# Routing slots by one-hot products, the first token gathers in the routing stage, and three embedding tiles and a prepared weight for the last stage of a hybrid transformer block

## The chip, the cores and the metric

One Trainium2 chip; the program runs on one of its cores. The metric is the device time of one execution in microseconds (us). The kernel before took 3019.23 us, the median of three executions (3015.76 to 3023.67). Each execution computes the whole block once, in float32 data, for 2048 tokens of width 1024.

## The reference

One layer of a decoder block: three token mixers side by side (a gated linear attention, a sparse attention that picks 256 keys, a sliding window), an output product, then a hierarchical mixture of experts, then a per-token embedding that is gated by the hidden state, and a last norm. The change touches only what follows the output product:

```python
h = h + hier_moe(rms_norm(h, g_ffn), ...)         # 4 groups of 8 experts, the best 2 in one group
e = rms_norm(p @ w_ple, g_ple)                    # p: 2048 x 256, w_ple: 256 x 1024
h = h + e * sigmoid(h @ w_ple_gate)               # w_ple_gate: 1024 x 1024
out = rms_norm(h, g_final)
```

Inside `hier_moe` each token's two expert choices are sorted by expert and every expert's tokens are padded to whole blocks of 128. `row` is the place of a (token, choice) pair in that padded list, and each block of 128 rows goes through `silu(xb @ w_gate[e]) * (xb @ w_up[e])` and then `@ w_down[e]`. The kernel so needs both directions of the map: from a token to its two rows (to fetch its results), and from a row to its token (to fetch its input, called its slot).

## The kernel before, in words

The program is a row of stages. Each is a block in which the five engines run their own instruction streams, tied by semaphores, and the stages are parted by a barrier of all engines. The last four are `mix` (output product, h and the normed f to memory, router logits), `route`, `experts` and `finish`. A tile is 128 tokens, so there are 16.

**route** (L1859 to L2118). VectorE (DVE) turns the logits into gates, into `rows` (L2089, a tile that holds each token's two rows) and then into `blocks`, the table of experts and counts that the later stages read into registers. TensorE (PE) ranks the tokens by two products with a triangle and with ones (L2019, L2020), between the products for tile 2 and tile 3 (`RANKED_AT`). Beside this, PE and ScalarE (ACT) compute the embedding `p @ w_ple` for all 16 tiles: PE turns a tile of p (L1996) and multiplies it (L2007), ACT squares the result for the norm (L1967), copies it (L1970) and stores it to `e_dram` (L1972). GpSimd (POOL) writes the slots by 32 indirect transfers (L1949) that scatter token numbers into `slots_dram`, one for each tile and choice, and it waits for all of them. SyncE (SP) loads p and the first experts' weights (`prefetch`, L2144 and L2149): gate and up for two experts and two down matrices, the second of which waits for the first to land.

**experts** (L2152 to L2431). For each block of 128 rows: POOL loads its slots from `slots_dram` (L2239), gathers 128 rows of f (L2247), PE turns them (L2311), ACT copies them to a rounded half, POOL makes the remainder (L2255), and PE does gate and up as three rounded products each (L2323 to L2325: high by high, low by high, high by low), then turns the hidden rows (L2332) and does down in full float32 (L2341). DVE splits each expert's gate and up into a rounded half `high` (L2232) and the remainder, in place, in `low` (L2234). The two buffers of `low` alternate by expert. The loop over blocks is a hardware loop whose count comes from `blocks`; `low` and `wd` are addressed there by a register. SP loads the next weights as buffers come free and at last `w_ple_gate` into `wg` (`load_next`, L2443).

**finish** (L2446 to L2661). It begins with ACT rounding `wg` to `wg_high` (L2592) and DVE making `wg_low` (L2647). For each tile: SP loads h and e, POOL gathers its two rows of results y (L2518), DVE adds them with their gates (L2611), PE turns the sum (L2546), ACT and DVE split it (L2576, L2620), PE does 48 products of 512 columns (L2558 to L2560), ACT takes the sigmoid (L2583), DVE multiplies and adds (L2633, L2635), ACT squares (L2588), POOL takes the inverse root, DVE scales (L2641) and SP stores. The order on PE is turn(0), turn(1), product(0), turn(2), product(1) and so on. Tile 0's products wait for all of tile 0's split, and each k of them for its slice of `wg_low`.

## Time and profile before

| | us |
|---|---|
| median of three executions | 3019.23 |
| the profiled execution | 3013.49 |
| its span, first to last instruction | 3011.8 |
| `mix` ends, `route` begins | 1705.0 |
| `route` ends, `experts` begins | 1791.4 |
| `experts` ends, `finish` begins | 2785.0 |
| PE busy in the span | 2668.7 (89%) |
| DVE, ACT, POOL busy | 1799.7, 1287.6, 985.0 |
| memory read and written | 331.69 MB, 107.53 MB |

The stage borders are read from the start of the first instructions of each stage in the trace. A span's engine share says little here, since each stage has its own limit: read the time at which a stage's last wait ends, what ended it, and what PE does in the first microseconds of the next stage.

### The profile page before, as it was taken

How to read it: one execution, taken by the hardware profiler on the slowest of the kernel's cores; microseconds unless marked ns; L12 is line 12 of the kernel's file. 1: busy time of each engine (PE TensorE's matmuls, PEld its weight loads, DVE VectorE, ACT ScalarE, POOL GpSimd, SP SyncE). 2: the span in 40 equal slices, each digit the busy share in tenths (PEclk: the TensorE clock that was granted, in tenths of full speed). 3: DMA queues.
4: the chain of work that ended last, by engine and by line, in shares of the span. 5: the costliest groups of instructions: out<-in, count | busy, mean ns of one | idle time of the engine just before them, and what ended most of it. 6: DMA issues, size and time to landing. Idle time of an engine off the chain costs nothing. (4 is left out here: it accounts for less than half of the span.)

```text
span 3011.8 us, 34857 instructions
## 1 busy us (share of the span) xinstructions
PE 2668.7 (89%) x11056; PEld 1674.1 (56%) x11057; DVE 1799.7 (60%) x2255; ACT 1287.6 (43%) x2377; POOL 985.0 (33%) x973
## 2 busy tenths in 40 slices
PE   6989789999947878888799869999999999998698
PEld 3634333444833434444588626666666666665587
DVE  2188999688876666766322346764564445740676
ACT  2377868839815556665222242222222222222222
POOL 1477887200011111121000054534544445441221
PEclk9999999999978989999799889999999999999799
DMA  5102211111141123212444486996596665971564
GB/s 154 50 29 52 33 34 39 56 56 54 39 129 57 43 65 104 67 50 91 179 146 148 179 206 242 325 361 211 204 346 219 216 218 205 347 282 42 206 227 140
DMA packets 224946, 440.79 MB, mean 146 GB/s; under 512 B 25704, under 2 KB 93864, under 8 KB 224696
## 3 DMA queue, kind: packets, MB, share of 16 engines
q1 hardware_dynamic: 199528, 357.78, 34.8%
q0 software_dynamic: 16080, 47.93, 5.1%
q10 hardware_dynamic: 9216, 33.56, 3.2%
q8 instruction: 63, 1.03, 0.1%
q14 instruction: 59, 0.48, 0.1%
HBM read 331.69 MB, written 107.53 MB: 146 GB/s over the span
## 5 line engine op out<-in xcount | busy, mean ns | idle before, releaser
L2232 DVE CAST p_high<-p_low 128x2048 fp32r<-128x2048 f32 x128 | 200.9, 1569 | 441.0 <-PE p_psG L2325 300.1
L625 PE MATMUL p_psP<-home,p_ring 128*128 128x512 f32 (+1 forms) x960 | 421.0, 597 | 0.0
L2341 PE MATMUL p_psY<-p_wd,p_hT 128*128 x768 | 337.9, 593 | 2.1 <-ACT p_hT L2401 1.9
L2234 DVE TENSOR_TENSOR p_low<-p_low,p_high 128x2048 fp32r<-128x2048 f32 x128 | 319.8, 2499 | 4.4
L625 PEld LDWEIGHTS p_psP<-home,p_ring 128*128 128x128 f32 (+1 forms) x960 | 175.4, 185 | 241.0 <-issue 240.8
L2261 POOL TENSOR_TENSOR p_hid<-p_act_g,p_act_u 128x512 f32<-128x512 f32 x48 | 62.0, 1292 | 528.3 <-ACT p_act_u L2396 276.2
L2341 PEld LDWEIGHTS p_psY<-p_wd,p_hT 128*128 128x128 f32 x768 | 142.2, 190 | 163.7 <-issue 163.5
L654 PE MATMUL p_psI<-p_kI,p_qI 64*128 64x512 f32 (+3 forms) x608 | 147.8, 594 | 54.2 <-ACT p_relu L550 54.1
L2255 POOL TENSOR_TENSOR p_xT_low<-p_xT,p_xT_high 128x512 fp32r<-128x512 f32 x96 | 191.1, 2008 | 1.5 <-ACT p_xT L2386 1.5
L2323 PE MATMUL p_psG<-p_high,p_xT_high 128*128 128x512 f32 x384 | 170.7, 445 | 15.6 <-DVE p_low L2234 9.3
L698 DVE TENSOR_SCALAR_CACHE_REDUCE p_equal<-p_S_low,p_flip 128x512 uint8<-128x512 f32 (+4 forms) x139 | 168.6, 1213 | 0.0
L2323 PE MATMUL p_psU<-p_high,p_xT_high 128*128 128x512 f32 x384 | 157.4, 410 | 5.2 <-DVE p_low L2234 5.2
L564 ACT ACTIVATE p_relu<-p_relu,p_small 128x512 f32<-128x512 f32 (+3 forms) x266 | 161.4, 661 | 0.0
L550 ACT ACTIVATE p_relu<-p_psI 128x1024 f32<-128x1024 f32 (+3 forms) x152 | 136.7, 914 | 40.5 <-POOL p_S_high L481 14.6
L2407 ACT ACTIVATE p_y<-p_psY 128x512 f32<-128x512 f32 x96 | 57.4, 598 | 224.7 <-PE p_psY L2341 224.7
L2325 PE MATMUL p_psG<-p_high,p_xT_low 128*128 128x512 f32 x384 | 153.2, 399 | 0.0
L2324 PE MATMUL p_psG<-p_low,p_xT_high 128*128 x384 | 153.2, 399 | 0.0
L698 DVE TENSOR_SCALAR_CACHE_REDUCE p_above<-p_S_low,p_flip 128x384 uint8<-128x384 f32 (+4 forms) x139 | 150.5, 1083 | 3.3
L2324 PE MATMUL p_psU<-p_low,p_xT_high 128*128 x384 | 151.9, 396 | 0.0
L2325 PE MATMUL p_psU<-p_high,p_xT_low 128*128 128x512 f32 x384 | 151.8, 395 | 0.0
L1330 PE MATMUL p_psL<-p_kA,home 64*128 64x512 f32 (+3 forms) x320 | 85.1, 607 | 69.0 <-ACT home L1216 32.4
L1473 DVE SCALAR_TENSOR_TENSOR p_logits<-p_mask,p_psL 128x1024 f32<-128x1024 uint8 (+3 forms) x80 | 84.8, 1060 | 100.3 <-PE p_psL L1330 100.2
(374 smaller groups left out, 5610.4 us busy)
## 6 DMA issues: line engine op xcount, KB each, us to landing
p_low<-in_w_expert_gate_dram SPq DMA_DIRECT2D x32, 2048.0 KB, 13.7
p_low<-in_w_expert_up_dram SPq DMA_DIRECT2D x32, 2048.0 KB, 18.8
p_wd<-in_w_expert_down_dram SPq DMA_DIRECT2D x32, 2048.0 KB, 10.9
y_dram<-p_y ACTq DMA_DIRECT2D x48, 512.0 KB, 7.9
p_xt<-in_x_dram SPq DMA_DIRECT2D x32, 512.0 KB, 4.5
y_dram<-p_clear SPq DMA_DIRECT2D x32, 512.0 KB, 4.6
proj_f<-p_stage SPq DMA_DIRECT2D x52, 256.0 KB, 2.3
p_ot<-o_dram SPq DMA_DIRECT2D x16, 512.0 KB, 4.1
```

Source lines behind the costliest of these rows:

```text
L550: act.activation(relu[:, n % NRELU, :, 0:c1 - c0], psI[:, n % NI, :, 0:c1 - c0], ACT.Relu).then_inc(relu_done, 1)
L564: act.activation(dst, src, ACT.Copy, scale=small[:, j, h:h + 1]).then_inc(weighed, 1)
L625: mm = pe.matmul(psP[0:n, i % 2, :], w, aT[:, k, c * CH:(c + 1) * CH], start=k == 0, stop=k == KD - 1)
L654: mm = pe.matmul(psI[:, n % NI, half, 0:c1 - c0], qI[r, b % 2, i, :], kI[r, c0:c1], start=True, stop=True)
L698: return dve.tensor_scalar((above, equal)[jj % 2][:, 0:W], scores_of(S_low, S_high, j), value, None, ALU.is_ge, ALU.add, accum_out=cnt[:, ...
L2232: dve.tensor_copy(high[:, m, k, :], low[:, par, m, k, :].bitcast(F32)).then_inc(high_done, 1)
L2234: dve.tensor_tensor(low[:, par, m, k, :], low[:, par, m, k, :].bitcast(F32), high[:, m, k, :].bitcast(F32), ALU.subtract).then_inc(w_split, 1)
L2255: pool.tensor_tensor(xT_low[:, k, :], xT[:, k, :], xT_high[:, k, :].bitcast(F32), ALU.subtract).then_inc(xT_split, 1)
L2323: pe.matmul(ps[:, :], xT_high[:, k, :], high[:, m, k, :], start=k == 0, stop=False)
L2324: pe.matmul(ps[:, :], xT_high[:, k, :], left, start=False, stop=False)
L2325: mm = pe.matmul(ps[:, :], xT_low[:, k, :], high[:, m, k, :], start=False, stop=k == KD - 1)
L2341: mm = pe.matmul(psY[:, c, :], hT[:, par, k, :], wd[:, bass.ds(at, 1), k, c * CH:(c + 1) * CH].rearrange("p a f -> p (a f)"), start=k == 0 ...
```

## The change

Five things move (L2026, L2115, L2275 and L2765 are lines of the changed kernel).

- **Slots.** The scatter and its memory are gone. DVE makes, from `rows`, for each tile and choice a one-hot of the row inside its block (128 wide) and a one-hot of its block (66 wide) times the token number, both float16. PE multiplies and sums them (L2026): 16 products of 66 columns after the embedding product of the sixth tile it handles and 16 after the seventh (`PLACED_BESIDE`). DVE copies the sum to `slots` (L2115), ahead of its work on `blocks`. In the expert stage POOL copies a column of it in place of the load from memory.
- **First gathers.** The gathers of blocks 0 and 1 are issued by POOL in `route`, as soon as `slots` is there.
- **Three tiles' embedding.** `route` computes tiles 3 to 15 only (`OWN = 3`), and `finish` computes tiles 0 to 2 at its start, straight into its buffer `e`. Their p, `w_ple` and g_ple are loaded late in `experts` (`load_tail`), as is h of tile 0.
- **Prepared weight.** DVE rounds `wg` at the end of `experts` (L2275) into the first buffer of `low`; `finish` begins with DVE making the remainder (L2765) in the second. PE reads both through registers.
- **Loads.** The second up matrix waits for nine embedding tiles, and the second down matrix goes to the start of `experts`.

In `finish`, half of product(0) now comes ahead of turn(1).

```diff
-                sp.dma_start(pt[:, b * TPC:(b + 1) * TPC, :], p[0, 0, b * CH:(b + 1) * CH, :].rearrange("(j p) n -> p j n", p=P)).then_inc(p_loaded[b], 16)
+                t0, t1 = max(b * TPC, OWN), (b + 1) * TPC
+                sp.dma_start(pt[:, t0:t1, :], p[0, 0, t0 * P:t1 * P, :].rearrange("(j p) n -> p j n", p=P)).then_inc(p_loaded[b], 16)
                 if b == 0:
                     sp.dma_start(wp[:, :, :], w_ple[0].rearrange("(k p) n -> p k n", p=P)).then_inc(wp_loaded, 16)
-            prefetch(sp)
+            prefetch(sp, e_copied)
...
-            pool.dma_start(slots_dram.rearrange("(p n) a -> p (n a)", p=P), zeros[:, :]).then_inc(zeroed, 16)
-            pool.wait_ge(zeroed, 16)
-            pool.wait_ge(step, ROWS_AT)
-            for j in range(NT):
-                for c in range(2):
-                    pool.indirect_dma_start(out=slots_dram, out_offset=bass.IndirectOffsetOnAxis(ap=rows[:, c, j:j + 1], axis=0),
-                                            in_=token[:, j:j + 1], in_offset=None).then_inc(scattered, 16)
-            pool.wait_ge(scattered, 16 * 2 * NT)
+            for par in range(2):
+                pool.wait_ge(step, SLOTS_AT)
+                pool.indirect_dma_start(out=xb[:, par, :], out_offset=None, in_=f_dram,
+                                        in_offset=bass.IndirectOffsetOnAxis(ap=slots[:, par:par + 1], axis=0)).then_inc(x_loaded[par], 16)
...
+                if t - OWN in PLACED_BESIDE:
+
+                    c = PLACED_BESIDE.index(t - OWN)
+                    pe.wait_ge(step, PLACED_AT[c])
+                    for j in range(NT):
+                        mm = pe.matmul(psB[:, 0:NBX], in_block[:, c, j, :], of_block[:, c, j, :], start=(c, j) == (0, 0), stop=(c, j) == (1, NT - 1))
+                    mm.then_inc(slotted, 1)
...
+            after(tsc(row_i[:, 0, :, :], rows[:, :, :], BLK - 1, None, ALU.bitwise_and))
+            after(tsc(row_i[:, 1, :, :], rows[:, :, :], 7, None, ALU.arith_shift_right))
+            after(dve.tensor_copy(row_f[:, :, :, :], row_i[:, :, :, :]))
+            for c in range(2):
+                after(tt(in_block[:, c, :, :], over(iota[:, :], NT, 1), over(row_f[:, 0, c, :], P, 2), ALU.is_equal))
+                after(tt(of_block[:, c, :, :], over(iota[:, 0:NBX], NT, 1), over(row_f[:, 1, c, :], NBX, 2), ALU.is_equal))
+                after(tt(of_block[:, c, :, :], of_block[:, c, :, :], over(token_f[:, :], NBX, 2), ALU.mult))
+                assert n == PLACED_AT[c]
...
-            after(tt(cmpb[:, :, :], over(full[:, :], NBX, 1), over(iota[:, :], NE, 2), ALU.is_le))
+            dve.wait_ge(slotted, 2)
+            after(dve.tensor_copy(slots[:, :], psB[:, 0:NBX]))
+            assert n == SLOTS_AT
+            after(tt(cmpb[:, :, :], over(full[:, :], NBX, 1), over(iota[:, 0:NBX], NE, 2), ALU.is_le))
...
-BOTH_AT = 5 + 5 + 3 + 5 + 2 + 5 + 1
+BOTH_AT = 6 + 5 + 3 + 5 + 2 + 5 + 1
 R_AT = BOTH_AT + 1
 ROWS_AT = R_AT + 4 + 10 + 4 + 1
-
-RANKED_AT = 2
+PLACED_AT = (ROWS_AT + 6, ROWS_AT + 9)
+SLOTS_AT = ROWS_AT + 9 + 6
+
+RANKED_AT, PLACED_BESIDE = 1, (5, 6)
+
+OWN = 3
...
+            sp.wait_ge(d_loaded, 16)
+            load_down(sp, weights, 1, 1, w_down)
...
+            used = sp.value_load(blocks[0:1, NBX + 1 + NE:NBX + 2 + NE], min_val=0, max_val=NBLK)
+            twice = sp.snap(used * 2 + 4)
+            sp.wait_ge(y_done, twice)
+            load_tail(sp)
...
+            for k in range(KD):
+                dve.wait_ge(wg_loaded, 16 * KD)
+                dve.tensor_copy(wg_high[:, k, :], wg[:, k, :]).then_inc(wg_split, 1)
+            dve.wait_ge(wg_split, KD)
...
-                pool.dma_start(slot[:, par:par + 1], slots_dram[ts(b, BLK), :]).then_inc(slot_loaded[par], 16)
+                pool.tensor_copy(slot[:, par:par + 1], slots[:, bass.ds(b, 1)]).then_inc(slot_set[par], 1)
 
             def gather(b, par, it, turns, carried):
-                pool.wait_ge(slot_loaded[par], it * 16 + 16)
-                if turns is not None:
-                    pool.wait_ge(turned, turns)
+                pool.wait_ge(slot_set[par], it)
+                pool.wait_ge(turned, turns)
...
-            load_slots(0, 0)
-            load_slots(1, 1)
-            gather(0, 0, 0, None, 1)
-            gather(1, 1, 0, None, 2)
-            pool.wait_ge(x_loaded[0], 16)
+
+            pool.sem_inc(carrier_set, 2)
             load_slots(2, 0)
...
+def load_tail(sp, weights, p, w_ple, g_ple):
+    wp, ptail, gp, _, _, _ = tail_places(weights)
+    _, (w_loaded, h_loaded, tail_loaded) = weights
+    sp.dma_start(wp, w_ple[0].rearrange("(k p) n -> p k n", p=P)).then_inc(tail_loaded, 16)
+    sp.dma_start(ptail, p[0, 0, 0:OWN * P, :].rearrange("(j p) n -> p j n", p=P)).then_inc(tail_loaded, 16)
+    sp.dma_start(gp, row_broadcast(g_ple, D)).then_inc(tail_loaded, 16)
+    sp.wait_ge(w_loaded, 16 * KD)
+    sp.wait_ge(h_loaded, 16)
+    sp.wait_ge(tail_loaded, 48)
...
+            pool.wait_ge(own_squared, OWN)
...
+            first = pe.value_load(blocks[0:1, NBLK + 3:NBLK + 4], min_val=0, max_val=1)
+            second = pe.snap((first + 1) % 2)
+
+            def turn_p(i):
+
+                if i >= 2:
+                    pe.wait_ge(pT_done, i - 1)
+                for k in range(KP):
+                    mm = pe.transpose(psG[:, 1, i % 2, k * P:(k + 1) * P], ptail[:, i, k * P:(k + 1) * P], ident[:, :])
+                mm.then_inc(p_turned, 1)
+
+            def embed(i):
+                pe.wait_ge(pT_done, i + 1)
+                if i >= 2:
+                    pe.wait_ge(own_copied, i - 1)
+                for c in range(2):
+                    ps = (psE[:, c, :], psG[:, 0, c, :])[i % 2]
+                    for k in range(KP):
+                        mm = pe.matmul(ps, pT[:, i % 2, k, :], wp[:, k, c * CH:(c + 1) * CH], start=k == 0, stop=k == KP - 1)
+                mm.then_inc(own_done, 1)
+
+            def product(t, halves=(0, 1)):
                 pe.wait_ge(hT_done, 2 * t + 2)
+                if t == 0:
+                    pe.wait_ge(own_copied, OWN)
                 if t >= 2:
                     pe.wait_ge(sig_done, 2 * (t - 1))
-                for c in range(2):
-                    part = slice(c * CH, (c + 1) * CH)
+                for c in halves:
                     for k in range(KD):
                         if (t, c) == (0, 0):
                             pe.wait_ge(w_split, k + 1)
-                        pe.matmul(psG[:, t % 2, c, :], hT_high[:, t % 2, k, :], wg_high[:, k, part], start=k == 0, stop=False)
-                        pe.matmul(psG[:, t % 2, c, :], hT_high[:, t % 2, k, :], wg_low[:, k, part], start=False, stop=False)
-                        mm = pe.matmul(psG[:, t % 2, c, :], hT_low[:, t % 2, k, :], wg_high[:, k, part], start=False, stop=k == KD - 1)
+                        w_high, w_low = (low_gu[:, bass.ds(i, 1), k // 4, k % 4 * 2 + c, :].rearrange("p a f -> p (a f)") for i in (first, second))
+                        pe.matmul(psG[:, t % 2, c, :], hT_high[:, t % 2, k, :], w_high, start=k == 0, stop=False)
+                        pe.matmul(psG[:, t % 2, c, :], hT_high[:, t % 2, k, :], w_low, start=False, stop=False)
+                        mm = pe.matmul(psG[:, t % 2, c, :], hT_low[:, t % 2, k, :], w_high, start=False, stop=k == KD - 1)
                     mm.then_inc(g_done, 1)
 
+            turn_p(0)
+            for i in range(OWN):
+                if i + 1 < OWN:
+                    turn_p(i + 1)
+                embed(i)
             turn(0)
-            for t in range(NT):
+            product(0, (0,))
+            turn(1)
+            product(0, (1,))
+            for t in range(1, NT):
                 if t + 1 < NT:
                     turn(t + 1)
                 product(t)
 
...
+            for k in range(KD):
+                dve.tensor_tensor(wg_low[:, k, :], wg[:, k, :], wg_high[:, k, :].bitcast(F32), ALU.subtract).then_inc(w_split, 1)
             add(0)
-            dve.wait_ge(w_loaded, 16 * KD)
-            for k in range(KD):
-                dve.wait_ge(high_done, k + 1)
-                dve.tensor_tensor(wg_low[:, k, :], wg[:, k, :], wg_high[:, k, :].bitcast(F32), ALU.subtract).then_inc(w_split, 1)
             low(0)
...
+                def prefetch(sp, e_copied):
                     for e in range(2):
                         load_gate_up(sp, weights, GATE, e, e, w_expert_gate)
+                        if e == 1:
+
+                            sp.wait_ge(e_copied, NT - OWN - 4)
                         load_gate_up(sp, weights, UP, e, e, w_expert_up)
                     load_down(sp, weights, 0, 0, w_expert_down)
-                    sp.wait_ge(weights[3], 16)
-                    load_down(sp, weights, 1, 1, w_expert_down)
-
-                route(nc, outer, router, slots_dram, gates, rows, blocks, ident, prefetch, p, w_ple, e_dram, e_squares)
```

The diff does not show how the work of an engine now lines up, so three places follow as the compiled programs have them.

PE in `route`, before, around the ranking (L1996 turns a tile of p, L2007 multiplies it, L2019 and L2020 rank):

```order
L2007 MATMUL p_psE<-p_wp,p_pT 128x512 x4
L2019 MATMUL p_psA<-p_both,p_before 128x512
L2020 MATMUL p_psB<-p_both,p_ones 128x512
L1996 MATMUL p_psT<-ident,p_pt 128x128 x2
L2007 MATMUL p_psE<-p_wp,p_pT 128x512 x4
L1996 MATMUL p_psT<-ident,p_pt 128x128 x2
L2007 MATMUL p_psE<-p_wp,p_pT 128x512 x4
```

PE in `route`, changed, where the slots are made (L2026; here p stands in `p_wg`):

```order
L2007 MATMUL p_psE<-p_wp,p_pT 128x512 x4
L1996 MATMUL p_psT<-ident,p_wg 128x128 x2
L2007 MATMUL p_psE<-p_wp,p_pT 128x512 x4
L2026 MATMUL p_psB<-p_of_block,p_cmpb 128x66 x16
L1996 MATMUL p_psT<-ident,p_wg 128x128 x2
L2007 MATMUL p_psE<-p_wp,p_pT 128x512 x4
L2026 MATMUL p_psB<-p_of_block,p_cmpb 128x66 x16
```

The ranking comes one tile of work earlier, after the second product, and 16 small products now stand behind each of the sixth and seventh.

PE at the start of `finish`, before (L2546 turns the sum, L2558 to L2560 are the 48 products of a tile):

```order
L2546 MATMUL p_psT<-ident,p_hs 128x128 x16
L2558 MATMUL p_psG<-p_wg_high,p_hT_high 128x512
L2559 MATMUL p_psG<-p_wg_low,p_hT_high 128x512
L2560 MATMUL p_psG<-p_wg_high,p_hT_low 128x512
L2558 MATMUL p_psG<-p_wg_high,p_hT_high 128x512
L2559 MATMUL p_psG<-p_wg_low,p_hT_high 128x512
L2560 MATMUL p_psG<-p_wg_high,p_hT_low 128x512
L2558 MATMUL p_psG<-p_wg_high,p_hT_high 128x512
```

PE at the start of `finish`, changed (L2627 and L2637 are the embedding of tiles 0 to 2, L2615 turns the sum, L2651 to L2653 are the products; ISA is register work):

```order
L2619 TENSOR_LOAD blocks
L2619 ISA x2
L2627 MATMUL p_psG<-ident,p_wd 128x128 x4
L2637 MATMUL p_psE<-p_wd 128x512 x4
L2627 MATMUL p_psG<-ident,p_wd 128x128 x2
L2637 MATMUL p_psG<-p_wd 128x512 x4
L2637 MATMUL p_psE<-p_wd 128x512 x4
L2615 MATMUL p_psT<-ident,p_hs 128x128 x8
L2651 ISA
L2651 MATMUL p_psG<-p_low,p_hT_high 128x512
L2652 ISA
L2652 MATMUL p_psG<-p_low,p_hT_high 128x512
```

Three tiles of embedding stand ahead of the first turn, and only one tile is turned ahead of the first products. The register work stands ahead of tile 0's products alone.

DVE at the start of `finish`, before, and then changed, there with its last work of `experts` (L2275 rounds, L2647 and L2765 make the remainder, L2611 and L2727 add the results, L2620 and L2736 split):

```order
L2611 SCALAR_TENSOR_TENSOR p_ht<-p_y,gates,p_ht 128x1024
L2611 SCALAR_TENSOR_TENSOR p_hs<-p_y,gates,p_ht 128x1024
L2647 TENSOR_TENSOR p_wg_low<-p_wg,p_wg_high 128x1024 x8
L2620 TENSOR_TENSOR p_hT_low<-p_psT,p_hT_high 128x512 x2
L2611 SCALAR_TENSOR_TENSOR p_ht<-p_y,gates,p_ht 128x1024
L2611 SCALAR_TENSOR_TENSOR p_hs<-p_y,gates,p_ht 128x1024
```

```order
L2275 CAST p_low<-p_wg 128x1024 x8
L2765 TENSOR_TENSOR p_low<-p_wg,p_low 128x1024 x8
L2727 SCALAR_TENSOR_TENSOR p_first_h<-p_y,gates,p_first_h 128x1024
L2727 SCALAR_TENSOR_TENSOR p_hs<-p_y,gates,p_first_h 128x1024
L2736 TENSOR_TENSOR p_hT_low<-p_psT,p_hT_high 128x512 x2
L2727 SCALAR_TENSOR_TENSOR p_wd<-p_y,gates,p_wd 128x1024
L2727 SCALAR_TENSOR_TENSOR p_hs<-p_y,gates,p_wd 128x1024
```

The rounding moved into the stage before, and the remainder now comes ahead of the first addition.

## Rows read from the trace of the kernel before

**Rows 1.** Windows: start:end length, busy PE, PEld, DVE, ACT, POOL (instructions), clock, DMA share, GB/s.

```profile
1752.00:1791.00 39.00, 22.45 (x59) 9.73 (x57) 0.00 (x0) 16.88 (x26) 20.73 (x22) 0.83 0.94 186
...
1830.00:2700.00 870.00, 855.01 (x3316) 576.84 (x3315) 472.92 (x238) 211.12 (x392) 383.71 (x261) 1.00 0.74 267
```

**Rows 2.** Timeline of DVE in `route`: start, duration, engine, line, operation.

```profile
1736.14 0.18 DVE L2089 CAST rows<-p_rowf 128x32 int32<-128x32 f32 x1
...
1737.40 2.36 DVE L2098 TENSOR_TENSOR p_cmpb<-p_full,p_iota 128x2112 f32<-128x2112 f32 x1
```

**Rows 3.** Timeline of POOL, first and last scatter (32 in all), first of `experts`.

```profile
1737.24 1.08 POOL L1949 DMA_INDIRECT slots_dram<-p_token,rows  x1 [30.09 <-DVE p_full L2096]
...
1778.18 0.96 POOL L1949 DMA_INDIRECT slots_dram<-p_token,rows  x1 [0.30 <-issue]
1791.46 0.10 POOL L2263 MEMSET p_carrier<- 128x2 f32 x1 [12.32 <-POOLq L1865]
```

**Rows 4.** Timeline of PE in `route` (two records to a float32 product).

```profile
1711.55 5.93 PE L2007 MATMUL p_psE<-p_wp,p_pT 128*128 128x512 f32 x8 [1.95 <-DMA p_wp<-in_w_ple_dram]
...
1737.52 3.60 PE L2007 MATMUL p_psE<-p_wp,p_pT 128*128 128x512 f32 x8
...
1741.17 3.60 PE L2007 MATMUL p_psE<-p_wp,p_pT 128*128 128x512 f32 x8
```

**Rows 5.** ACT in `route`; then landing times of e_dram stores, 1730:1745 and 1777:1779.

```profile
1774.88 1.02 ACT L1967 ACTIVATE p_emb<-p_psE 128x1024 f32<-128x1024 f32 x1 [1.62 <-PE p_psE L2007]
...
1777.08 0.33 ACTq L1972 DMA_DIRECT2D e_dram<-p_emb  x1
...
DMA to landing us min/median/max: 6.2/7.9/10.9
...
DMA to landing us min/median/max: 12.6/12.6/12.6
```

**Rows 6.** Timeline of DVE and PE at the start of `experts`.

```profile
1792.83 1.34 DVE L2232 CAST p_high<-p_low 128x2048 fp32r<-128x2048 f32 x1 [41.48 <-issue]
...
1804.59 3.23 DVE L2234 TENSOR_TENSOR p_low<-p_low,p_high 128x2048 fp32r<-128x2048 f32 x1
...
1801.83 1.97 PE L2311 MATMUL p_psX<-ident,p_xb 128*128 128x128 f32 x8 [26.99 <-DMA p_xb<-f_dram,p_slot]
...
1805.83 0.77 PE L2323 MATMUL p_psG<-p_high,p_xT_high 128*128 128x512 f32 x1 [2.02 <-POOL p_xT_low L2255]
...
1819.76 1.04 PE L2311 MATMUL p_psX<-ident,p_xb 128*128 128x128 f32 x8
```

**Rows 7.** Tile p_xb; ACT's last store of `experts`, its landing, SP's first of `finish`.

```profile
L2247 POOL DMA_INDIRECT p_xb<-f_dram,p_slot x48: 1017/1830/3384, 1796.7 to 2722.9; - x48
...
2773.95 0.34 ACTq L2410 DMA_DIRECT2D y_dram<-p_y  x1
...
DMA to landing us min/median/max: 2.6/2.6/2.6
...
2785.03 0.81 SPq L2488 DMA_DIRECT2D p_ht<-h_dram  x2
```

**Rows 8.** Start of `finish`: chain that ended last (start, duration), and DVE (timeline).

```profile
2787.03 10.14 DMA p_y<-y_dram,rows
...
2799.80 9.16 DVE L2647 TENSOR_TENSOR p_wg_low<-p_wg,p_wg_high 128x1024 fp32r<-128x1024 f32 x8
...
2827.51 0.87 PE p_psT L2546 x8
```

**Rows 9.** PE in `experts` (timeline, 22 steps), in `finish` (chain, 47 steps).

```profile
2745.20 0.39 PE L2324 MATMUL p_psG<-p_low,p_xT_high 128*128 x1
...
2750.33 0.40 PE L2325 MATMUL p_psG<-p_high,p_xT_low 128*128 128x512 f32 x1
...
2851.93 0.23 PE p_psG L2558
...
2862.60 0.23 PE p_psG L2560
```

210 lines of the change are left out of this document (121 added, 89 removed).

## The prediction

> **What bounds the kernel now.** I read the stretches first, then the timeline of each engine around the three borders of the last stages, then the chain of waits at the start of the last one. The reader is to see that PE decides almost everywhere and that it stands still at the borders. In the middle of `experts` PE is busy for 855.01 of 870 us at full clock [rows 1], so nothing that the change does to slot loads or to DVE there can move more than a few us. In `finish` one tile follows the other without a gap on PE [rows 9]. What the change can win is PE's idle time at the borders, and in the 39 us before `experts` PE is busy for only 22.45 [rows 1].
>
> *Border one, route to experts.* `rows` is written at 1736.3 [rows 2]. POOL issues its first scatter at 1737.24 and its last, the 32nd, at 1778.18, one each 1.3 us [rows 3]. ACT's last store goes out at 1777.08 and lands 12.6 us later, at 1789.7 [rows 5]. So two things end `route` together, and `experts` begins at 1791.46 [rows 3].
>
> *Border two, the first block.* PE can turn block 0 only at 1801.83, when slots and then f have come from memory, and it starts its products at 1805.83. It is done with gate and up at 1819.76 [rows 6], 28.3 us after the stage began.
>
> *Border three, experts to finish.* The last store goes out at 2773.95 and lands after 2.6 us, at 2776.6. Yet SP's first transfer of `finish` starts at 2785.03 [rows 7]: 8.4 us in which no engine works.
>
> *Border four, the first tile.* The gather lands at 2797.17 and DVE makes the remainder from 2799.80, 9.16 us long, only after tile 0's addition. PE is done with tile 0 at 2827.51 [rows 8], 42.5 us after the stage began.
>
> **The change part by part.**
>
> *Routing, minus 14.0 us.* PE handles 13 tiles. Its first product ends at 1717.3 and each further tile takes 3.65 us [rows 4]: 12 of them give 1761.1. The ranking, which it keeps, took 1.7 us between two tiles. The 32 one-hot products have 66 columns and one pass. One record of an embedding product with 512 columns takes 0.45 us [rows 4], so each of the 32 lies between 66/512 of that (0.06) and 0.45. I take 0.1, near the end that the columns give: 3.2 us. PE also waits for DVE. The ranking comes one tile earlier, so `rows` is there at about 1733. Per choice DVE then writes 2048, 1056 and 1056 elements. 2112 take 2.36 us [rows 2], so this is 4.8 us, and both are there at 1738.7 and 1743.6, against PE's sixth product at 1738.0: 0.7 us of waiting. PE ends at 1766.5. From PE's end to ACT's store went 2.2 us [rows 5], a little more with the wake-up: 1769. The store's landing took 6.2 to 10.9 us in the middle of `route` and 12.6 at the end [rows 5], when scatters and the second down matrix were under way, both now gone. I take 8: 1777. With 0.5 for the barrier, `experts` begins at 1777.5, not 1791.5. The bounds are 16 us (landing in 6.2) and 3 (each one-hot product 0.45, which adds 11). POOL's two gathers start at about 1746 and land long before. DVE's work on `blocks` now ends at about 1760, hidden under PE's embedding. The up matrix that waits for nine tiles goes out at about 1755. Behind it on SP's queue is only a down matrix, and both are 4.2 MB against 20 us: hidden. If that cover goes, expert 1's split is late next.
>
> *First block, minus 7.0 us.* x is there, so turning starts about 1.7 us in, and the first product 4.0 us later as before [rows 6]. The next limit is DVE's split of expert 0. It starts 1.4 us in and ended 16.4 us in (1804.59 plus 3.23) [rows 6]. It now runs beside POOL's own split: the operation that did so took 3.23 us, against 2.36 of its kind in `route` [rows 2, 6], so I add 2 us for the two or three more that do. Then PE needs one more half of up, 12 products at 0.233 or 2.8 us: 21.3 us in, against 28.3. Bounds: 4 and 9.
>
> *Border three, minus 4.0 us.* What fills the 8.4 us the profile does not name. POOL issued 97 transfers in that stage (49 slot loads and 48 gathers [rows 7]), and is the engine that the barrier waits for. `route` with 33 of them has 1.8 us between the last landing and the next stage [rows 3, 5]. If the gap grows with them, the 46 that stay leave 4.0. I take 4.4 as left. Bounds: nothing won, and 6.
>
> *First tile, minus 8.5 us.* The remainder now runs first, 9.2 us, and the gather lands about then, so the addition ends at about 12. But PE must first do the three embedding tiles. The first product after idling took 5.93 us, not 3.60 [rows 4]: 1.5 to read its register, 1.4 for turning, then 5.9, 3.6 and 3.6 end at 16.1. ACT's square and copy add 2.2 [rows 5], its copy of h and DVE's split about 1.8: products start 20.1 us in. 48 of them and one turn are 12.2. After idling a product lost 2.3 us (5.93 less 3.60 [rows 4]); this pause is only some 3 us, and I add 1.6: 33.9 us, against 42.5. This term rests on ACT's chain, not on y. Bounds: 5 and 11.
>
> *Register operands in finish, plus 4.8 us.* All 768 products of `finish` now take the weight through a register, on the same tile as in `experts`. There 22 steps took 5.13 us, 0.2332 each. In `finish` 47 took 10.67, 0.2270 each [rows 9]. 768 times the difference is 4.8. That the difference comes from the register is not shown: even the products of `experts` without one step at 0.233. Bounds: 0 and 4.8.
>
> The Trainium skill (TensorE: Matmul & The Clock Gate, "Wait — 56ns, not 53.3ns?") says that back-to-back matmuls of one width step alike at full clock whichever decode path issues them. By that the register would cost nothing and the sum would be 33.5, not 28.7. It gives 215.7 ns for 512 columns, and neither stage here shows that.
>
> The sum is 14.0 + 7.0 + 4.0 + 8.5 - 4.8 = 28.7 us. Against the profiled execution's 3013.5 that gives 2984.8. The median of the runs shown lies 5.7 higher, so the median of the changed kernel would be 2990.5.
>
> **The rivals.**
>
> *Register free.* Everything as above, but `finish` steps at 0.227: 2985.7. For it: the matmuls of `experts` differ from those of `finish` in more than the register. Against: the nearest row is the one with it [rows 9].
>
> *Transfers hold the end of route.* The two loads that now start at 1755 meet the last four stores, and the last one still takes 12.6 us or more. 8 us less are won: 2998.5. For it: late stores were slower than early ones [rows 5]. Against: the stage has one 2 MB load and three stores less to move, and the scatter is gone.
>
> *The gains hide each other.* The borders move, but PE at once meets the next wait: DVE's split takes all of the 7 us, the slow clock and ACT all of the 8.5, the gap at border three stays. Then 14.0 - 4.8 = 9.2 are left: 3010, or a few us more with the bounds. For it: each border has a second wait within 10 us. Against: the ones at the first tile are worked out above.
>
> *Slower: the register in front of each product.* If resolving it holds the array by 0.06 us at each of the 768, that costs 46 us and the kernel ends at about 3032. It decides from 33.5/768 = 0.044 us on. For it: the compiled program has register work ahead of tile 0's products. Against: it has none ahead of the others, and in `experts`, where it stands ahead of every third, the step is 0.233 [rows 9].
>
> **How the numbers follow.** Chances: the forecast 0.47, register free 0.30, transfers 0.14, gains hidden 0.05, slower 0.03, and 0.01 for something else. The range takes in the first three with the bounds of their terms, 2979 to 3003; beyond lie about 2 in 10. A change under 0.3% (9 us) can't be told from none here. The first three cases are faster by more: with the hidden gains in the middle class this makes 0.92, 0.05 and 0.03.
>
> **What would show it right or wrong.** `experts` begins near 1777.5 and its first block is through gate and up some 21 us later. Between the last landing of `experts` and the first transfer of `finish` lie about 4 us. Tile 0's 48 products end some 34 us into `finish`. The step there is 0.233 or 0.227, which decides the first two cases. A first PE product of `finish` that starts later than 22 us in, or stores that land after 12 us, would make it wrong.

## The result, and the profile after

| | before | changed |
|---|---|---|
| median (range), four runs each, us | 3017.55 (3015.76 to 3023.67) | 2979.28 (2976.71 to 2984.45) |
| profiled execution, us | 3013.49 | 2976.71 |
| span, granted TensorE clock | 3011.8, 0.951 | 2975.0, 0.958 |
| PE busy | 2668.7 (89%) | 2673.1 (90%) |

The ratio is 0.9876, with a 95% interval from 0.9853 to 0.9899. The changed kernel is faster by 38 us in the medians and by 36.8 us in the two spans, where 28.7 were forecast.

Not all of that is the change. The stages ahead of `route` are the same code, yet `route` begins at 1704.9 us in the one trace and at 1699.9 in the other. The 14 traces of this study, one for each kernel below, whose code up to that place is the same or differs by an unused pad, have it anywhere from 1699.8 to 1716.1. So I count from the start of `route` to the end. That takes 1306.9 us before and 1275.1 after: **31.8 us were won**, and this is the number that the forecast must be held against. The stages from `route` on scatter too, though less, as the table of the experiments shows.

Stages of the changed kernel, as windows (start:end length, busy PE, PEld, DVE, ACT, POOL, clock, DMA share, GB/s):

```profile
1699.90:1769.60 69.70, 53.06 (x166) 24.43 (x166) 46.53 (x82) 33.13 (x54) 5.55 (x10) 0.89 0.83 303
1769.60:2754.00 984.40, 949.86 (x3648) 639.30 (x3648) 520.00 (x264) 234.59 (x433) 422.22 (x284) 0.99 0.69 251
2754.00:2975.00 221.00, 208.28 (x926) 164.87 (x926) 151.93 (x168) 61.97 (x109) 55.89 (x67) 0.97 0.56 183
```

`route`, `experts` and `finish` took 86.5, 993.6 and 226.8 us before; they take 69.7, 984.4 and 221.0 now. The rows that answer to [rows 2 to 5] are the timeline of the changed `route`, PE's one-hot products first, then POOL and ACT:

```profile
1733.74 0.68 PE L2026 MATMUL p_psB<-p_of_block,p_cmpb 128*128 128x66 f16 x16 [0.83 <-DVE p_of_block L2105]
1734.26 0.41 PE L1996 MATMUL p_psT<-ident,p_wg 128*128 128x128 f32 x2
...
1738.65 0.69 PE L2026 MATMUL p_psB<-p_of_block,p_cmpb 128*128 128x66 f16 x16 [0.54 <-DVE p_of_block L2105]
...
1754.04 7.03 PE L2007 MATMUL p_psE<-p_wp,p_pT 128*128 128x512 f32 x16
...
1740.19 3.10 POOL L1949 DMA_INDIRECT p_xb<-f_dram,router  x1 [38.80 <-DVE router L2115]
1743.59 0.97 POOL L1949 DMA_INDIRECT p_xb<-f_dram,router  x1 [0.30 <-issue]
1769.56 0.10 POOL L2304 MEMSET p_carrier<- 128x2 f32 x1 [25.00 <-POOLq L1866]
...
1763.31 0.33 ACTq L1972 DMA_DIRECT2D e_dram<-p_wg  x1
```

Sixteen one-hot products hold PE for 0.52 us, until the next record starts: 0.033 us each. The last scatter of [rows 3] is gone from the end of the stage. What ends it now is ACT's last store: it goes out at 1763.31, and the next stage begins 0.5 us after it has landed. Its landing took 5.8 us, the last number of this row of the transfers:

```profile
e_dram<-p_wg ACTq DMA_DIRECT2D x1, 512.0 KB, 5.8
```

The first block [rows 6] and the end of `experts` [rows 7], as timeline rows of the changed kernel (the row of DVE is its last split ahead of the last half of block 0's products):

```profile
1771.41 1.94 PE L2349 MATMUL p_psX<-ident,p_xb 128*128 128x128 f32 x8 [10.34 <-PEq L2338]
1775.76 0.76 PE L2361 MATMUL p_psG<-p_high,p_xT_high 128*128 128x512 f32 x1 [2.41 <-POOL p_xT_low L2296]
...
1784.62 2.29 DVE L2271 TENSOR_TENSOR p_low<-p_low,p_high 128x2048 fp32r<-128x2048 f32 x1
...
1786.96 0.50 PE L2361 MATMUL p_psU<-p_high,p_xT_high 128*128 128x512 f32 x1 [0.40 <-DVE p_low L2271]
...
1789.86 1.04 PE L2349 MATMUL p_psX<-ident,p_xb 128*128 128x128 f32 x8
...
2746.79 0.34 ACTq L2448 DMA_DIRECT2D y_dram<-p_y  x1
2754.00 0.34 SPq L2562 DMA_DIRECT2D p_wd<-h_dram  x1
```

From the second turn (1789.86) PE's path goes on as before: 947.2 us to the start of the last block's down products, 946.2 before. From the last y store to `finish` it is 7.2 us instead of 11.1. The start of `finish` [rows 8], timeline:

```profile
2755.88 5.11 PE L2637 MATMUL p_psE<-p_wd 128*128 128x512 f32 x8
...
2769.25 1.02 ACT L2683 ACTIVATE p_e<-p_psE 128x1024 f32<-128x1024 f32 x1
2772.23 0.66 PE L2651 MATMUL p_psG<-p_low,p_hT_high 128*128 x1 [3.29 <-DVE p_hT_low L2736]
```

The embedding is off PE by 2768 and off ACT at 2770.3; the first product follows 18.2 us into the stage, and tile 0 is done 32.1 us in. The step of the products there [rows 9] is read from two rows of the chain, 42 products apart: 9.80 / 42 = 0.2333 us.

```profile
2800.22 0.23 PE p_psG L2653
...
2810.02 0.23 PE p_psG L2653
```

### The profile page after: what moved, and what is told of

Read it like the earlier page. It is cut to its first block and busy times, and to the rows that moved or that the text cites. A ratio compares the mean times of both kernels' runs of the same rounds, so it can differ in the third digit from the quotient of the medians.

```text
span 2975.0 us, 34899 instructions
## 1 busy us (share of the span) xinstructions
PE 2673.1 (90%) x11088; PEld 1675.0 (56%) x11089; DVE 1818.3 (61%) x2274; ACT 1279.4 (43%) x2369; POOL 952.3 (32%) x935
## 6 DMA issues: line engine op xcount, KB each, us to landing
p_low<-in_w_expert_up_dram SPq DMA_DIRECT2D x32, 2048.0 KB, 18.1
```

## The experiments

Times in the table are in us, counted from the start of their stage or from the event named, each from one trace of the kernel. "To the end" is from the start of `route`. "Second turn" is PE's second turn of x in `experts`; "store to finish" is from the last y store's issue to SyncE's first transfer; "first product" is that of tile 0. From the start of the last block's down products (16 records, two to a product) to the last y store go 8.0 us in some executions and 9.7 in others, whatever the kernel. In both cases PE has just waited 1.9 us; in the changed kernel the granted clock is 0.57 to 0.58 from 2738 to 2742, partly the lower level of 1.2 GHz, and in the kernel before it stays at 1.00. So differences under 2 us in a stage are not read by themselves.

| kernel | route | second turn | store to finish | experts | first product | finish | to the end |
|---|---|---|---|---|---|---|---|
| before | 86.5 | 28.3 | 11.1 | 993.6 | 29.3 | 226.8 | 1306.9 |
| changed | 69.7 | 20.3 | 7.2 | 984.4 | 18.2 | 221.0 | 1275.1 |
| b_reg | 85.2 | 27.3 | 11.1 | 996.5 | 29.1 | 225.9 | 1307.6 |
| b_offsets | 86.2 | 27.4 | 11.1 | 994.0 | 29.7 | 231.4 | 1311.6 |
| b_offsets2 | 83.1 | 27.8 | 11.1 | 994.5 | 29.7 | 230.1 | 1307.8 |
| a_high | 69.9 | 20.3 | 7.2 | 982.1 | 17.1 | 219.8 | 1271.9 |
| a_late_wait | 64.2 | 20.5 | 6.9 | 983.2 | 18.4 | 221.2 | 1268.5 |
| a_drain_early | 69.4 | 20.3 | 3.4 | 980.1 | 18.6 | 221.3 | 1270.9 |
| a_dma48 | 70.4 | 20.4 | 11.1 | 988.7 | 18.1 | 220.8 | 1279.8 |
| a_own0 | 80.2 | 20.3 | 6.9 | 981.4 | 16.7 | 219.9 | 1281.5 |
| a_gather_in | 70.1 | 27.9 | 7.4 | 989.1 | 19.2 | 221.9 | 1281.1 |
| a_round_late | 69.6 | 20.3 | 7.2 | 984.6 | 24.8 | 227.5 | 1281.7 |
| a_align | 69.3 | 20.3 | 7.2 | 975.8 | 17.9 | 215.9 | 1261.0 |
| best2 | 64.1 | 20.6 | 3.4 | 973.8 | 18.0 | 216.1 | 1254.0 |

The kernel before, b_reg, b_offsets and b_offsets2 have the same code in `route`, and it takes 83.1 to 86.5 us; in the seven kernels whose end of `route` and number of tiles are those of the change it takes 69.3 to 70.4. Between single traces, a difference of up to 3 us in the old `route` is therefore scatter.

### Is it the register? b_reg and a_high

b_reg, on the kernel before:

```diff
-wg_high, wg_low = sb("wg_high", [P, KD, D], F32R), sb("wg_low", [P, KD, D], F32R)
+pair = sb("pair", [P, 2, KD, D], F32R)
+w_high, w_low = (pair[:, bass.ds(i, 1), k, part].rearrange("p a f -> p (a f)") for i in (first, second))
```

> The kernel before, with one edit: the rounded weights and their remainder lie in one tile, and the 768 products of finish address them through a register, as in the changed kernel. Theory (the register makes the step): finish steps at 0.2332 us instead of 0.2270, so it takes 226.8 + 4.8 = 231.6 us, and the kernel is 4.8 us slower, 0.16%. Rival one (something else in the changed kernel's last stage makes the step: the tile, or how the weights lie in it): the step stays at 0.2270 and finish at 226.8. Rival two (the register stands in front of each product, 0.044 us or more): 34 us or more are added. The stages ahead of route should begin and end as before; if route begins at another time than 1704.9 us, that difference is the scatter of one execution to the next.

a_high, on the changed kernel (the tile `high` is allocated ahead of `route`, some scratch of `route` moves into `wd`):

```diff
-w_high, w_low = (low_gu[:, bass.ds(i, 1), k // 4, k % 4 * 2 + c, :].rearrange("p a f -> p (a f)") for i in (first, second))
+w_high, w_low = (w[:, k, c * CH:(c + 1) * CH] for w in (wg_high, wg_low))
```

> The changed kernel, with the rounded weights of the last stage in the experts' tile high and the remainder in a tile of its own, both addressed without a register; DVE's eight roundings at the end of experts wait for the last up product. Theory (the register makes the step): the step in finish is 0.2270 instead of 0.2332 us, so finish takes 221.1 - 4.8 = 216.3 us; the roundings (5.1 us) lie under PE's last 16 down products (8.8 us) and experts stays at 984.4: 4.8 us faster than the changed kernel in all, about 2974. Rival (the place and layout of the weights make it): step 0.2332, finish 221.1. If the roundings are not hidden, experts grows by up to 5 us instead.

The chain of b_reg in `finish`, from the second to the last product of a tile, 46 steps in 10.44 us, 0.2270 each:

```profile
2861.30 0.23 PE p_psG L2564
...
2871.74 0.23 PE p_psG L2565
```

and of a_high, the same 46 steps in 10.73 us, 0.2333:

```profile
2808.08 0.23 PE p_psG L2648
...
2818.81 0.23 PE p_psG L2649
```

With the register the kernel before keeps its short step, and its time: 3015.72 us against 3013.40, ratio 1.0005 (0.9991 to 1.0018). Without it the changed kernel keeps its long one: 2986.74 us, ratio 0.9914 (0.9891 to 0.9938). From `route` to the end it is 3.2 us shorter than the changed kernel, 1.7 of it in the last block's down products and none in the step. The register costs nothing that these runs can tell (step 0.2269 us with it and without), and my theory fell. What the prediction drew from the Trainium skill (TensorE: Matmul & The Clock Gate, "Wait — 56ns, not 53.3ns?"), that the step does not depend on how a matmul is decoded, agrees with b_reg, though b_reg changes how the operand is addressed and not how the instruction is decoded.

### Where the operands lie: b_offsets, b_offsets2, a_align

b_offsets and b_offsets2 put unused pads between tiles of the kernel before, as here ahead of the last stage's weights:

```diff
+sb("pad", [P, 8])
 wg_high, wg_low = sb("wg_high", [P, KD, D], F32R), sb("wg_low", [P, KD, D], F32R)
+sb("pad2", [P, 24])
```

> The register made no difference: with it the last stage of the kernel before still steps at 0.2267 us, and without it the changed kernel's last stage still steps at 0.2333. What is left is where the operands lie. By their byte offset in a partition, modulo 128, the moving weights and the stationary activations stand at (32, 32) in mix, step 0.2267; at (0, 0) in finish of the kernel before, 0.2267; at (96, 0) in experts and in finish of the changed kernel, 0.2333. This kernel is the one before with unused pads between its tiles: mix at (96, 96), experts at (96, 32), finish at (32, 0). Theory A (the moving operand at 96 is slow): mix 0.2333, experts 0.2333, finish 0.2267. Theory B (the two operands must agree modulo 64): mix 0.2267, experts 0.2267, finish 0.2333. Theory C (the place does not matter, something else in the stage does): mix 0.2267, experts 0.2333, finish 0.2267.

> Six stages so far step at 0.227 us where the moving and the stationary operand have the same offset modulo 128 bytes, (0, 0), (32, 32), (96, 96), and at 0.233 where not, (96, 0), (96, 32), (32, 0). The kernel before with other pads: mix at (32, 96), which agree modulo 64 only; experts at (32, 32) and finish at (0, 0) modulo 128, both with operands 128 apart modulo 512. Theory (agreement modulo 128 decides): mix 0.233, experts mostly 0.227 with a mean of about 0.229 as in the aligned kernel, finish 0.227. Rival one (modulo 64 decides, and experts is slow for another reason): mix 0.227. Rival two (modulo 512 decides): mix, experts and finish all 0.233.

a_align, on the changed kernel (`slot` and `half` also move behind the large tiles of their stages):

```diff
+sb("p8_pad", [8])
 wg, first_h = sb("p8_wg", [KD, D]), sb("p8_first_h", [D])
```

> The changed kernel, with a pad of 32 unused bytes ahead of its weights and two small tiles moved behind the large ones, so that in experts and finish every operand of a product stands at a multiple of 128 bytes. Theory (the offset makes the step): 0.2267 us in both stages: 2304 products of experts and 768 of finish gain 0.0066 each, 15 and 5 us, less what DVE and GpSimd then hold up in experts: the kernel 15 to 20 us faster than the changed one, about 2960. Rival (the stage, not the offset): 0.2333 in both and no gain.

The steps, with the operands' offsets in a partition as the program places them, modulo 512 bytes. Each step is the mean time from one record to the next over a whole stage, stops left out: some 730 pairs in `mix` and in `finish`, some 2040 in `experts`.

| stage, kernel | moving, stationary | step, us |
|---|---|---|
| mix, before | 32, 32 | 0.2275 |
| mix, b_offsets | 96, 96 | 0.2275 |
| finish, before and b_reg | 256, 256 | 0.2269 |
| finish, a_align | 256, 256 | 0.2269 |
| experts, a_align | 256, 256 | 0.2291 |
| finish, changed and a_high | 224, 256 | 0.2333 |
| experts, before and changed | 224, 256 | 0.2331 |
| mix, b_offsets2 | 32, 96 | 0.2333 |
| experts, b_offsets | 224, 288 | 0.2332 |
| experts, b_offsets2 | 288, 416 | 0.2328 |
| finish, b_offsets | 288, 384 | 0.2342 |
| finish, b_offsets2 | 0, 128 | 0.2323 |

Mix of b_offsets2 in its timeline, 18 steps in 4.20 us:

```profile
1644.75 0.39 PE L1742 MATMUL p_psM<-p_w_high,p_oT_high 128*128 128x512 f32 x1
...
1648.95 0.39 PE L1742 MATMUL p_psM<-p_w_high,p_oT_high 128*128 128x512 f32 x1
```

and of b_offsets, 18 steps in 4.08 us:

```profile
1641.85 0.39 PE L1743 MATMUL p_psM<-p_w_low,p_oT_high 128*128 128x512 f32 x1
...
1645.93 0.39 PE L1743 MATMUL p_psM<-p_w_low,p_oT_high 128*128 128x512 f32 x1
```

b_offsets struck down all three of its theories: `mix` with the moving operand at 96 is fast (against A), `experts` at (96, 32), which agree modulo 64, is slow (against B), and `finish` became slow by pads alone (against C, that the place does not matter). A further one, agreement modulo 128, fell with b_offsets2, whose `finish` agrees modulo 128 and not modulo 512, and is slow: its second rival came true. The same row shows that multiples of 128, which a_align aimed at, are not what counts. What all twelve rows obey: **the step is short where both operands have the same offset modulo 512 bytes, and long where they differ, by 32, 64, 96 or 128**. A difference of 256 was not tried, so the rows can't tell agreement modulo 512 from agreement modulo 256. Why it is so stays open, and so does why `experts` in a_align has its short step only from the eleventh of 24 products on (means of 0.227 to 0.229 there, 0.225 to 0.235 ahead of it). The stage times agree with the steps: `finish` takes 231.4 us in b_offsets and 230.1 in b_offsets2, against 226.8. The two kernels took 3017.47 and 3019.65 us, one run each.

In a_align `finish` falls by 5.1 us, `experts` by 8.6, where 15 were expected: the ten slow products of each 24 keep its mean step at 0.2291, which gives 9.2 us in 2304 products. The chain of its `finish` answers to the changed kernel's, 46 steps in 10.44 us, 0.2270:

```profile
2817.52 0.23 PE p_psG L2653
...
2827.96 0.23 PE p_psG L2654
```

The runs: 2973.87 us (2965.34 to 2978.87), ratio 0.9847 (0.9821 to 0.9873). That interval overlaps with the changed kernel's; the stages, 14.1 us shorter from `route` to the end, are the better evidence.

### GpSimd's share of border three: a_dma48 and a_drain_early

a_dma48 and a_drain_early, each on the changed kernel:

```diff
 pool.tensor_copy(slot[:, par:par + 1], slots[:, bass.ds(b, 1)]).then_inc(slot_set[par], 1)
+pool.dma_start(extra[:, par:par + 1], f_dram[0:P, 0:1], allow_slow_non_contiguous=True).then_inc(extra_loaded[par], 16)
```

(in a_dma48 GpSimd also waits for the added transfers, ahead of each gather and at the end), and

```diff
-pool.wait_ge(y_stored[par], m * 16 + 32)
+act.wait_ge(y_stored[par], m * 16 + 32)
+act.activation(act_g[:, par:par + 1], act_u[:, par:par + 1], ACT.Copy)
```

> The changed kernel, with one more transfer of 128 x 4 bytes by GpSimd per block of experts, as many as the slot loads that the change removed (about 48). Theory (GpSimd's closing instruction grows with the number of its transfers in the stage): it takes about 7.9 us instead of 3.8, and from the last y store's issue to finish go 11.3 us instead of 7.2. Rival (the gap shrank because the slot loads' short transfers from DRAM are gone from the end of the stage, or by the barrier's own luck): 3.8 and 7.2 stay. The slower split of GpSimd may cost PE a little in the loop in either case.

> The changed kernel, with the wait for the last two y stores at the end of experts moved from GpSimd to ScalarE, so that GpSimd leaves the stage about 20 us earlier. Theory (the 3.8 us between the last landing and finish are GpSimd's closing instruction, which runs only after its last wait and grows with its transfers): it now runs under PE's last products, and the gap between the last y landing and the first transfer of finish falls from about 4.1 us to below 1: experts 984.4 to about 981, the kernel 3 to 4 us faster than the changed one. Rival (the gap is a fixed cost of the barrier, or waits for transfers to be quiet, whoever waits): the gap stays at 4.

Last y store and SyncE's first transfer of `finish`, in a_dma48:

```profile
2754.64 0.34 ACTq L2453 DMA_DIRECT2D y_dram<-p_y  x1
...
2765.73 0.34 SPq L2567 DMA_DIRECT2D p_wd<-h_dram  x1
```

and in a_drain_early:

```profile
2754.96 0.34 ACTq L2446 DMA_DIRECT2D y_dram<-p_y  x1
...
2758.35 0.34 SPq L2563 DMA_DIRECT2D p_wd<-h_dram  x1
```

11.1 us with the transfers put back, 3.4 with GpSimd gone early, 7.2 as the change has it. The views leave out GpSimd's instruction that closes a stage (a DRAIN); the trace records it. In `experts` it took 7.98 us before (97 transfers by GpSimd), 3.82 after (46) and 7.67 in a_dma48 (93). In a_drain_early it took 4.70 and ran from 2737.3 to 2742.0, under PE's last products. Both theories of this border hold for `experts`, as expected. From stage to stage the number of transfers does not give the length: it is 0.68 us in `mix` and 2.44 in the stage ahead of it, both without a transfer, 3.30 in `finish` with 32, and 11.30 in the changed `route`, whose two gathers it spans; there it ends 18 us before ACT is done and costs nothing. In `route` before, it is what ended the stage: it ran 2.76 us and ended at 1791.21, after ACT was through at 1789.97, and in the three other traces of that code it was last as well. a_dma48 took 2988.26 us in its one run, a_drain_early 2984.71 (2981.38 to 2990.51), ratio 0.9913 (0.9887 to 0.9939). So the whole times do not show a gain over the changed kernel. In the trace `route` begins at 1708.8, 8.9 us later than in the changed kernel's, and from there it is 4.2 us shorter; the gain rests on this trace and on best2's, with the same 3.4 us.

### What ends route: a_late_wait and a_own0

a_late_wait takes the first two lines from the end of ACT's part of `route` and puts the other two ahead of `load_next(sp)` in `experts`:

```diff
-for b in range(4):
-    act.wait_ge(e_stored[b], 16 * len(range(OWN + b, NT, 4)))
+for b in range(4):
+    sp.wait_ge(e_stored[b], 16 * len(range(OWN + b, NT, 4)))
```

> The changed kernel, with the wait for the last four e stores taken from ACT at the end of route and put on SyncE in experts, ahead of the first transfer that overwrites their source. Theory (the end of route is PE, ACT and then the landing of the last store, nothing else): route takes 69.7 - 5.5 = 64.2 us, x and the weights of expert 0 are there, and the first block is through gate and up 20.4 us into experts as now: 5.5 us faster in all, about 2974. Rival (transfers hold what comes next anyway): the 5.5 us come back as idle time of PE or DVE in the first block, which then ends about 26 us into experts, and the time stays.

a_own0 sets OWN to 0 and lets SyncE load the first three e tiles in `finish`:

```diff
-OWN = 3
+OWN = 0
+for t in range(OWN, NS):
+    sp.dma_start(e[:, t % NS, :], e_dram[ts(t, P), :]).then_inc(e_loaded[t % NS], 16)
```

> The changed kernel, with all 16 embedding tiles in route and the first three read back by finish, as in the kernel before; slots by one-hot products, gathers in route, early rounding and the waits stay. Theory: route grows by three tiles at 3.65 us, 11.0, to 80.6, and finish loses ACT's and PE's embedding ahead of the first product: its first product starts no longer 18.2 us in but when DVE's remainder, the addition and its split are done, about 15, 3 to 4 us earlier. Sum: 7 to 8 us slower than the changed kernel. Rival (the embedding ahead of tile 0 is hidden under DVE's remainder and the gather): finish keeps 221 us and the whole 11.0 are lost. Rival two (route's end is set by something else than its tiles): route grows by less than 8.

The end of `route` in a_late_wait:

```profile
1765.50 0.33 ACTq L1971 DMA_DIRECT2D e_dram<-p_wg  x1
...
1766.28 0.10 POOL L2303 MEMSET p_carrier<- 128x2 f32 x1 [19.55 <-POOLq L1866]
```

`experts` now begins 0.8 us after the last store's issue, and the second turn comes 20.5 us later, as before the edit: in this trace nothing takes the 5.5 us back, and best2's `route` takes 64.1 us too. The whole time, 2975.06 us (2972.34 to 2981.17), ratio 0.9881 (0.9856 to 0.9907), is too close to the changed kernel's to show them. In a_own0 `route` is 10.5 us longer, as three tiles at 3.65 say, and `finish` only 1.1 shorter: its first product starts 16.7 us in instead of 18.2. I had expected 3 to 4. So the embedding ahead of tile 0 is nearly hidden under DVE's remainder and the gather. Without it DVE waits 1.4 us for the gather once the remainder is made, and PE, idle until then, turns the sum in 1.97 us at a granted clock of 0.50, where the changed kernel needs 1.04 at 1.00. Moving three tiles was worth 9.4 us net of these two stages (6.4 from `route` to the end: a_own0's `experts` happens to be 3.0 shorter, 1.7 of it in the last block's down products). The one run took 2994.50 us.

### The first block and the early rounding: a_gather_in and a_round_late

a_gather_in moves the two `pool.indirect_dma_start(out=xb[:, par, :], ...)` from `route` to GpSimd's start in `experts`. a_round_late takes the roundings from DVE's end of `experts` and puts them back at ACT's start of `finish`:

```diff
-dve.tensor_copy(wg_high[:, k, :], wg[:, k, :]).then_inc(wg_split, 1)
+act.activation(wg_high[:, k, :], wg[:, k, :], ACT.Copy).then_inc(high_done, 1)
```

> The changed kernel, with the two first gathers issued at the start of experts and not in route; the slots still come from the one-hot products. Theory (x is what the first block waits for once it is late): PE turns block 0 about 7 us into the stage instead of 1.85, and the second turn, 20.3 us in now, comes 4 to 6 us later: 24.5 to 26. The kernel is then 4 to 6 us slower than the changed one, and the rest of the 8 us between the two kernels came from the slots. Rival (DVE's split of expert 0 sets the first block anyway): the second turn stays at 20.3.

> The changed kernel, with the eight roundings of the last stage's weights taken from DVE in experts and put back on ACT at the start of finish, ahead of its part of the three embedding tiles. Theory (the first tile rests on ACT's chain): 7.7 us of rounding stand ahead of that chain; the first product of tile 0 starts 26 us into finish instead of 18.2, and finish takes 228 to 229 us instead of 220.9; experts stays at 984. Rival (y's gather and DVE's remainder set the first product): it starts no later than 20, and finish grows by 2 at most.

POOL at the start of `experts` in a_gather_in:

```profile
1776.51 0.10 POOL L2300 MEMSET p_carrier<- 128x2 f32 x1 [68.61 <-POOLq L1866]
1777.51 1.74 POOL L2305 DMA_INDIRECT p_xb<-f_dram,router  x1 [0.90 <-POOLq L2303]
1779.55 3.15 POOL L2305 DMA_INDIRECT p_xb<-f_dram,router  x1 [0.30 <-issue]
```

PE's first turn comes 10.1 us in, where 7 were expected, and the second 27.9, where I expected 24.5 to 26. So nearly the whole gain of the first block, 28.3 to 20.3, hangs on the early gathers. It does not follow that fetching the slots from DRAM cost nothing. Here the first gather goes out 1.0 us into the stage; in the kernel before it went out 5.3 us in (the first time in the row of p_xb of [rows 7]), once the slots had landed and GpSimd had handled them. But there the two gathers landed in 5.1 and 5.2 us, and here in 9.1 and 8.3: the change also put the load of the second down matrix at the start of `experts`, at 1776.51 in this trace, and the DMA share from 1779 to 1786 is 1.01, against 0.01 from 1791.4 to 1798 before. The 4 us won by the slots and the 4 lost to that load cancel; no run parts them.

In a_round_late ACT's eight roundings take 7.68 us, and the first product starts at 24.8 instead of 18.2 (26 expected):

```profile
2756.66 7.68 ACT L2700 ACTIVATE p_low<-p_wg 128x1024 fp32r<-128x1024 f32 x8 [7.45 <-PEq L2186]
```

With the embedding in place, the early rounding is worth 6.6 of the 10.4 us of the first tile. a_gather_in took 2989.23 us and a_round_late 2985.84, one run each.

### The three edits together: best2

> The changed kernel with the three edits that won time in their own stages: operands at multiples of 128 bytes, the e stores awaited by SyncE late in experts, the last y stores awaited by ScalarE. Theory (they add): route 64.2 us, experts 984.4 - 8.6 - 3.8 = 972.0, finish 215.9: 23 us less than the changed kernel, about 2957. Rival (they share a cover: once PE runs faster, DVE's split or the weights' transfers take the gain back): 10 us or less.

2964.37 us (2958.49 to 2967.68, five runs), ratio 0.9827 (0.9803 to 0.9850), below the interval of the changed kernel. From `route` to the end it takes 1254.0 us, 21.1 less than the changed kernel where 23 were expected: the edits add, less 1.8 us in `experts`, which is within what one trace differs from another there. It beats both kernels. Its stages, as windows (their borders stand up to 0.2 us early):

```profile
1708.50:1772.60 64.10, 53.59 (x166) 24.56 (x166) 46.54 (x82) 33.17 (x54) 5.52 (x9) 0.91 0.82 302
1772.60:2746.40 973.80, 943.43 (x3648) 639.77 (x3648) 521.18 (x264) 235.30 (x435) 425.41 (x284) 0.99 0.69 255
2746.40:2962.70 216.30, 203.42 (x926) 164.32 (x926) 151.88 (x168) 62.03 (x109) 55.92 (x67) 0.98 0.57 187
```

## Why the prediction was right, and where it was not

- **Direction and range** held, the range by luck: 2979.28 lies in 2979 to 3003, but 0.28 us from its edge, less than the scatter of the runs, and 11.2 us below the forecast median of 2990.5. The spans beat the sum of 28.7 by 8.1 us; 5.0 of these lie ahead of `route`, in code that the change leaves alone. Against the 31.8 won the sum was 3.1 short. That is smaller than its errors: the five terms below came to 34.2 us, 5.5 more than forecast, and 2.7 were given back in `experts`, 1.0 on PE's way to the last block's down products and 1.7 from there to the last y store; 0.3 is left over.
- **Routing, forecast −14.0, measured −16.8.** PE's end came out right, 61.6 us into the stage forecast and 61.2 measured, but errors in it cancel. The one-hot products were mis-sized: I took 0.1 us each, 3.2 us, and they take 0.033, 1.0 us, below the lower bound of 0.06. By my own terms PE's sixth product ends at 1737.3 and not at 1738.0, so PE waits 1.4 us for DVE and not 0.7 (it waited 0.83 and 0.54), and the terms as written add to 1766.7, not 1766.5. The first product ended 13.0 us in and not 12.3. The term that failed is the landing of the last store, 8 us forecast and 5.8 measured; the other 0.6 us lie in PE's and ACT's ends. All this is within the 3.4 us by which the old `route` scatters. The rival of the transfers that hold the end is refuted. What ended `route` before was GpSimd's closing instruction, 1.2 us after ACT, which the prediction did not have.
- **First block, −7.0, measured −8.0.** The mechanism was right, x on time: without it, in a_gather_in, the second turn is 7.6 us later. The second turn comes 20.3 us in and not 21.3, and the row of DVE above says why: its split of expert 0 ends 17.3 us in, not 18.4, and the last half of up starts then. I had added 2 us for operations beside POOL's to an end, 16.4, that already held one of them; the two that were slow here made it 0.9 later.
- **Border three, −4.0, measured −3.9.** The theory that the gap grows with GpSimd's transfers came from two rows only, of two stages, and as a rule over stages it does not hold; within `experts` a_dma48 doubles them and gets the old gap back.
- **First tile, −8.5, measured −10.4.** Products start 18.2 us in and not 20.1: PE began its embedding 1.9 us in, not 2.9, and the slow first eight records took 5.1 and not 5.9. The 1.5 us for reading the register had no row behind it; PE's first turn began 0.7 us in. That it rests on ACT's chain is half right. a_round_late (a longer chain) moves it by 6.6 us; a_own0 (none at all) by 1.5 only, since DVE's remainder, the gather and the addition come next.
- **Register operands, +4.8.** The size is right: 0.2269 became 0.2333, 4.9 us in 768 products. The cause is wrong. I read the step of `experts` as the register's, and it was the place of the tiles: the change put the weights where `experts` had them, 32 bytes off the activations modulo 512. So the forecast case came true in number while *register free* was true in mechanism. I had written that the rows do not show the cause, and gave both cases most of the chance.
- **Slower and gains hidden** did not happen: no border gave its gain back.

## What to carry to other kernels

Read a step that differs by 3% between stages as a question about where operands lie before you ask about instructions: a pad of 32 bytes, with two small tiles moved behind the large ones, gave 14 us here from `route` to the end (one trace), more than several of the change's own parts. Before you call a part worthless because taking it out costs nothing, look at what the rest of the change put in its place: the slots' 4 us and the down matrix's 4 us hid each other. Ask of each wait at the end of a stage who must really wait for it, and let an engine with many transfers behind it leave early. Count a change from the first instruction that it touches: over equal code two executions differed by up to 16 us.

## What the runs showed of the hardware that I had not expected

- The step of the rounded (float32r) products with 512 columns is 0.227 us with both operands at the same offset modulo 512 bytes and 0.232 to 0.234 with offsets that differ by 32, 64, 96 or 128, in every stage and kernel of the table above but for the first ten of each 24 products in `experts`.
- GpSimd's closing instruction of `experts` took 3.82 us with 46 transfers of GpSimd in the stage, 7.67 with 93 and 7.98 with 97. Over other stages the count does not order it: 0.68 and 2.44 with none, 2.76 with 33, 3.30 with 32, 11.30 around two gathers. It is in no view, and costs only where GpSimd leaves last.
- Sixteen one-hot products of 66 float16 columns held PE for 0.52 us, 0.033 us each, a third of what I took.
